# The mixer's input projection: latent blocks and short-convolution blocks in alternation

## What is computed

```python
for i in range(DEPTH):                      # DEPTH = 2
    x = x + 0.5 * swiglu(rmsnorm(x, ffn1_norm[i]), ...)
    h = rmsnorm(x, mix_norm[i]) @ w_in[i]
    y_mla = mla_mixer(h[..., OFF_Q:OFF_KV], h[..., OFF_KV:OFF_KPE], h[..., OFF_KPE:OFF_CONV], ...)
    y_conv = conformer_conv_mixer(h[..., OFF_CONV:OFF_HY], ...)
    y_hy = hyena_mixer(h[..., OFF_HY:], ...)
    y = concatenate([rmsnorm(y_mla, ..), rmsnorm(y_conv, ..), rmsnorm(y_hy, ..)])
    x = x + y @ w_out[i]
    x = x + 0.5 * swiglu(rmsnorm(x, ffn2_norm[i]), ...)
```

## Time and profile before

| what | value |
|---|---|
| median of 3 executions | 3376.35 us (3375.7 to 3377.36) |
| the profiled execution, its own time | 3375.04 us |
| its span, first to last instruction | 3373.2 us |
| mean granted clock of TensorE | 0.972 of full |
| TensorE busy | 3166.9 us, 94% |
| VectorE busy | 1591.3 us, 47% |
| POOL busy | 1881.0 us, 56% |
| ScalarE busy | 697.8 us, 21% |

### The profile page before, as it was taken

One profiled execution on the slowest core, in us unless ns is written; L12 is line 12 of the kernel. 1 busy time (PEld: TensorE's weight loads), 2 busy tenths in 40 slices (PEclk: granted clock), 3 DMA queues, 4 the chain that ended last, 5 costly groups with the idle time before them and its releaser, 6 DMA issues.

```text
span 3373.2 us, 39369 instructions
## 1 busy us (share of the span) xinstructions
PE 3166.9 (94%) x14296; PEld 2413.3 (72%) x14296; DVE 1591.3 (47%) x2395; ACT 697.8 (21%) x1377; POOL 1881.0 (56%) x2079
## 2 busy tenths in 40 slices
PE   6999889989999999998898899997999999999998
PEld 5888665457888788886454688885787666677786
DVE  4312497554312531226857432225665588753424
ACT  2101102251101110011114310013333444420101
POOL 5867670006767777776200377774674423267866
PEclk9999998999999999999899999998999999999999
DMA  3323230002323233233200123232332111123222
GB/s 119 109 84 100 75 123 35 7 1 88 103 91 97 85 99 102 92 100 110 72 7 1 50 88 106 88 100 75 121 92 93 51 45 45 32 76 105 95 87 75
DMA packets 67281, 263.17 MB, mean 78 GB/s; under 512 B 7390, under 2 KB 8606, under 8 KB 65856
## 3 DMA queue, kind: packets, MB, share of 16 engines
q1 hardware_dynamic: 61344, 238.86, 22.0%
q10 hardware_dynamic: 5792, 22.37, 1.8%
HBM read 259.10 MB, written 2.10 MB: 77 GB/s over the span
## 4 chain that ended last, share of the span: by engine, by line
PE 82%; DVE 13%; ACT 2%; issue 2%; POOL 0%; DMA 0%; ACTq 0%; DVEq 0%; SPq 0%; POOLq 0%
PE psum L525 22%; PE psum L527 21%; PE psum L526 21%; DVE y_conv L2046 3%; PE psum L864 2%; PE psum L879 2%; PE psum L822 2%; PE psum L602 1%; PE psum L678 1%; PE psum L628 1%; PE psum L694 1%; PE psum L543 1%; PE psum L756 1%; PE psum L696 1%; PE psum L698 1%
## 5 line engine op out<-in xcount | busy, mean ns | idle before, releaser
L494 POOL TENSOR_TENSOR w_lo<-w_raw,w_hi 128x256 fp32r<-128x256 f32 (+2 forms) x1660 | 1409.8, 880 | 34.6
L489 POOL TENSOR_SCALAR w_hi<-w_raw 128x1024 fp32r<-128x1024 f32 (+2 forms) x415 | 471.3, 1136 | 1435.3 <-PE psum L527 1223.3
L525 PE MATMUL psum<-u_hi,w_hi 128*128 128x512 f32 x2400 | 956.9, 399 | 40.8 <-DVE u_lo L1719 31.1
L526 PE MATMUL psum<-u_lo,w_hi 128*128 128x512 f32 x2400 | 943.8, 393 | 0.0
L527 PE MATMUL psum<-u_hi,w_lo 128*128 128x512 f32 x2400 | 943.4, 393 | 0.0
L525 PEld LDWEIGHTS psum<-u_hi,w_hi 128*128 128x128 f32 x2400 | 456.6, 190 | 169.1 <-issue 52.9
L527 PEld LDWEIGHTS psum<-u_hi,w_lo 128*128 128x128 f32 x2400 | 456.4, 190 | 97.4
L526 PEld LDWEIGHTS psum<-u_lo,w_hi 128*128 128x128 f32 x2400 | 457.5, 191 | 94.7 <-issue 2.9
L525 PE MATMUL psum<-h_hi,w_hi 128*128 128x512 f32 x960 | 374.1, 390 | 4.1 <-issue 4.1
L527 PE MATMUL psum<-h_hi,w_lo 128*128 128x512 f32 x960 | 373.5, 389 | 0.0
L526 PE MATMUL psum<-h_lo,w_hi 128*128 128x512 f32 x960 | 373.5, 389 | 0.0
(11 more groups left out here) (298 smaller groups left out, 3442.3 us busy)
## 6 DMA issues: line engine op xcount, KB each, us to landing
w_raw<-in_w SPq DMA_DIRECT2D x335, 512.0 KB, 3.4
w_raw<-in_w SPq DMA_DIRECT2D x48, 768.0 KB, 4.2
w_raw<-in_w SPq DMA_DIRECT2D x32, 640.0 KB, 3.8
dft<-in_dft ACTq DMA_DIRECT2D x2, 2048.0 KB, 12.6
idft<-in_idft ACTq DMA_DIRECT2D x2, 2048.0 KB, 7.8
w_c<-in_w_c ACTq DMA_DIRECT2D x2, 2048.0 KB
x<-in_xt SPq DMA_DIRECT2D x1, 2048.0 KB, 8.9
decay<-in_decay ACTq DMA_DIRECT2D x2, 1024.0 KB, 7.1
```

Of the source, the lines that this page charges most:

```text
L489: pool.tensor_scalar(hi, raw, 1.0, 1.0, ALU.mult, ALU.mult).then_inc(w_hi_ready, 1)
L494: ins = pool.tensor_tensor(lo[:, part], raw[:, part], hi[:, part].bitcast(F32), ALU.subtract)
L525: pe.matmul(out, hi[:, c, :], rhs_hi(c), start=(s == 0), stop=False)
L526: pe.matmul(out, hi[:, c, :], rhs_lo(c), start=False, stop=False)
```

## The change

A list `W_IN` gives the order of the 14 blocks. The first five stay, then blocks 8, 5, 9, 6, 10, 7 alternate, then 11, 12, 13. The list of loads, TensorE's loop, ScalarE's and VectorE's follow it; what is done with a block goes by its number k as before, what belongs to a place (the wait for the normalized input, the sines) goes by the place `at`. The weights stay where they are in memory.

```diff
+W_IN = (0, 1, 2, 3, 4, 8, 5, 9, 6, 10, 7, 11, 12, 13)
...
     for _ in range(DEPTH):
         ffn(PARTS, 2)
-        add(8, 14)
+        for k in W_IN:
+            out.append((8, first[8] + k, 1))
+        first[8] += len(W_IN)
         add(8, 8)
         ffn(PARTS, 2)
...
-                for k in range(14):
-                    of_u(u_arrives if k == 0 else None)
-                    if k in SINES:
-                        l = SINES.index(k)
+                for at, k in enumerate(W_IN):
+                    of_u(u_arrives if at == 0 else None)
+                    if at in SINES:
+                        l = SINES.index(at)
...
-                for k in range(14):
+                for at, k in enumerate(W_IN):
                     n, m = w.gemm()
                     if 2 <= k < 4:
...
-                    if k in SINES:
-                        l = SINES.index(k)
+                    if at in SINES:
+                        l = SINES.index(at)
...
-                for k in range(14):
+                for at, k in enumerate(W_IN):
                     n, m = w.gemm()
                     if k < 2:
...
-                    if k in SINES:
-                        l = SINES.index(k)
+                    if at in SINES:
+                        l = SINES.index(at)
```

## The result

The changed kernel takes 3382.01 us (median of 20 executions), the kernel before, beside it, 3375.68 (20): ratio 1.0017, with 1.0010 to 1.0024 as its 95% interval. Timed once more later it gave 1.0018 (1.0009 to 1.0027). Two of the 20 executions of the changed kernel were disturbed ones (4075.07 us at a granted clock of 0.742, 12221.04 at 0.423); the median of the other 18 is 3381.7. The change is slower by 0.17%, which lies in the predicted range (3374.0 to 3383.5), under the 0.2% that count here as a change, and on the side that was forecast, but at nearly three times the forecast size: about +6 us against +2.2. The profiled execution took 3380.86 us over a span of 3379.0, where before it took 3375.04 over 3373.2.

A forecast was written before the change was run, and what follows sets the result against it. The prediction took the input projection as a VectorE stage on the chain: +2.75 us of wait less 1.7 saved by overlap with POOL gives +1.1 a layer, +2.2 in all, for 3378.55 us, range 3374.0 to 3383.5.

The forecast's parts named there:

- Step (a): At place 5 VectorE needs a product where it ran six taps without a wait; it idles 2.75 us a layer, unhidden.
- (b): All other new product waits, at places 7, 9 and 11 to 13, are covered because VectorE stays behind TensorE; cost nothing.
- (d): TensorE's own end moves from 498.1 to about 499.5 us, with 12 us of cover before the first filter product; cost nothing.
- Step (c): ScalarE's copies of the latents queue behind the sines, before their banks are wanted by later products; cost nothing.
- Step (e): In the projection, 2.85 us more of POOL's work runs while VectorE can't be slowed by it; saves 1.7 us a layer.
- The first rival: Wait paid in full: taps slow by themselves, or POOL's splits slide; +2.75 us a layer, 3381.85 us, chance 12%.
- The prediction's price: In step (e), each us of POOL's work moved into the shade saves 0.59 us of VectorE's time beside taps.
- The third rival: Faster: the shade is near its upper bound, -1.8 us a layer, 3372.7 us or a little under; chance 4%.
- The second: Slower by TensorE's clock: its rise comes behind the products with ones, 4.0 us more a layer, 3386.5 us; chance 7%.

The follow-up runs named there:

- the change, TensorE's gap filled: Changed kernel with nine unused products in TensorE's gap ahead of its wait for the first sine: 3379.66 us, 1.0013 against the kernel before.
- alternation one block later: Changed kernel with block order 0 to 5, 8, 6, 9, 7, 10 to 13: 3374.94 us, 0.9998 against the kernel before.
- one tap into the wait: Changed kernel with one tap (two VectorE instructions) moved from behind place 5 to place 4, ahead of the wait: 3373.55 us, 0.9996 against the kernel before.
- one tap out of it: Changed kernel with one tap moved from place 4 to behind place 5's short convolution, lengthening the wait: 3381.08 us, 1.0017 against the kernel before.
- in pairs: Changed kernel with block order 0 to 5, 8, 9, 6, 7, 10 to 13: 3373.18 us, 0.9995 against the kernel before.
- the change again: Changed kernel timed once more with no edit: 3380.74 us, 1.0018 against the kernel before.
- before with TensorE's gaps filled: Kernel before with 12 unused products ahead of each of the third and fourth filter products: 3374.45 us, 1.0001 against the kernel before.
- the two doses: Changed kernel with one tap moved into the wait at place 5 (3373.55 us), or one moved out of it (3381.08 us).
- POOL's work cut: Three quarters of the low parts of the input projections' 28 blocks left out: 3358.86 us in the order before, 3365.98 in the changed one.
- pairs and eight: Order 0 to 5, 8, 9, 6, 7, 10 to 13, with one tap instead of two behind each of places 10 to 13: 3361.61 us, 0.9958.

## Why the prediction was right, and where it was off

The frame held: the projection is VectorE's stage, both layers alike, and what happens in it passes on to the end.

Step (a), the wait of 2.75 us at place 5, measured 2.77 and 2.73; the run with one tap in its place shows that it is the cause. Steps (b) and (d): no other product was waited for. TensorE's last block ended near 501.6 instead of 499.5, since place 8 ran at 0.77 of the clock and two later blocks waited for POOL; the cover was over 11 us and still enough. Step (c): each latent was copied 0.5 us behind its sine's start, and no product waited for ScalarE's copy.

Step (e) is where the stretch was mis-sized. It got 1.7 us saved a layer; measured is the wait less the growth, 2.77 - 1.84 = 0.93. The term that failed is its count of the shade, that is of POOL's work done while VectorE idles or reads PSUM. Step (e) had 8.9 us before and 11.75 after. Counted the same way from the two timelines of each run, it was 9.0 and 9.5, so 0.5 us more and not 2.85:

- The wait: 2.0 and not 2.75. Beside an idle VectorE POOL needed 3.59 us for four quarters and not 4.49, was done at 439.6, and stood idle for 0.90 until 440.5.
- The first sine's head (its first instruction, out of PSUM): 0.1 and not 0.5, as POOL waited until 447.2.
- The block near 460: nothing instead of 1.4, as POOL stood still until 463.3.
- The third sine's head: nothing instead of 0.8, as POOL's pause lasted until 483.9.
- Against these, the fifth short block had 2.3 and not 0.9, as POOL's last split came later. Smaller differences make up the rest.

The first rival had named this ("POOL's splits slide so that the shaded time is what it was"), at 12% together with slow taps; for the shade it is nearly what happened. The price of a microsecond in the shade was too low, which made up for part of it. The runs that have POOL's full work and all the taps in the stretch tell both terms apart:

| run | stretch less wait, layer 1 and 2, us | POOL's work in the shade, us |
|---|---|---|
| before | 80.2, 80.1 | 9.0, 9.1 |
| the change | 79.3, 79.1 | 9.5, 9.5 |
| the change, TensorE's gap filled | 78.8, 79.1 | 9.9, 9.7 |
| alternation one block later | 78.7, 78.7 | 10.2, 10.2 |
| one tap into the wait | 78.5, 78.6 | 10.7, 10.7 |
| one tap out of it | 78.1, 77.2 | 10.8, 11.9 |
| in pairs | 78.4, 78.1 | 11.0, 11.1 |

A straight line through these and the two runs left out (the change again, and before with TensorE's gaps filled) falls by 0.9 us for each us of shade and passes within 0.35 us of all of them; it was laid through the results afterwards. The prediction's price was 0.59. By the line the change's 0.5 us of shade give 0.4 of its 0.93; the rest is within the line's spread and stays open. The line also answers the two doses: filling the wait brought 1.2 us of shade besides, as the instructions out of PSUM then had 10.2 us of POOL's work beside them and not 7.5, and lengthening it brought 1.3 and 2.4.

Seen by groups of instructions, the taps gained 2.4 us and the sines lost 1.6. The order moved POOL's splits onto the sines, and step (e) treated everything but their heads as taps. Their one-source instructions in SBUF go from 0.42 us to as much as 1.18 beside POOL, a higher price than a tap's 0.69 to 1.2. How much of the price that was too low is theirs was not tested.

The checkpoints: sines ended at 453.95, 473.33 and 489.50, forecast 453.5, 473.5 and 489.7; the six taps behind the second took 4.52 us (forecast 4.2), those behind the third 6.76 (over 7); the first filter product was taken at 513.05, forecast 512.5. TensorE's waits ahead of the second and third sine's products:

```profile
454.79 1.04 PE L795 MATMUL psum<-f_h,f_w 64*64 64x512 f32 x2 [2.30 <-issue]
...
474.17 1.94 PE L795 MATMUL psum<-f_h,f_w 64*64 64x512 f32 x2 [5.63 <-issue]
```

The first as forecast (2), the second 5.6 and not 7.5, as the block before it came later by the lowered clock.

The rivals. The first (paid in full) did not happen to the stretch, which grew by 1.84 and not by 2.75. Its first mechanism is the rule of the Trainium skill (Vector Engine (DVE) Microarchitecture Reference, section Points that are easy to get wrong) that a scalar-tensor-tensor with two SBUF sources wider than bf16 halves the throughput. This case's traces do not agree: with POOL's work cut ten such taps took 7.99 us instead of 12.14, and alone four took 2.85. That the measured 3382.01 lies beside this rival's 3381.85 is chance, as it is made of other parts. The third rival (faster) had the shade near its upper bound of 16.6; it was 9.5.

The second, the clock in the products with ones, was priced at 4.0 us a layer and given 7%; it came at a tenth and a fifth of that, 0.40 and 0.86, and recurred. With 10.21 and 10.44 us these products lie outside the 9.5 to 10 that the prediction had named as a sign of being wrong. Together with the stretches (3.64 instead of 2.2) and the 0.9 us left over, this makes 5.8 instead of 2.2. The sign came out right by the mechanism that was forecast, the uncovered wait at place 5. The size did not, and that the time still lies in the range is owed to a range wide enough for the full wait and some clock; the term of the clock in the forecast itself was zero, and should not have been.

## What to carry to other kernels

On an engine that holds the chain, moving work that needs a product ahead of work that needs nothing costs about the wait for that product. It can be bought off with work that is already there: one tap moved turned 1.0017 into 0.9996. Where two engines slow each other, look at both timelines and count how much of the other's work falls beside idle time or instructions that it can't slow. In nine runs here that count went with the length of the stretch, and it can't be taken from the old timeline, since each wait moves the other engine's work. An instruction taken off the chain saved about what it takes alone (2.3 to 3.6 us for four, against 2.8), not what it took beside POOL. The larger gain was to do work where another engine holds the chain: 0.9958 for pairs and eight of the stretch's 87 instructions moved behind it, where the pairs alone gave 0.9995.

## What the runs showed of the hardware

Beside POOL's tensor instructions, most of VectorE's instructions with two SBUF sources took 1.1 to 1.2 us instead of 0.7 to 0.75, those with one SBUF source and one SBUF result 0.82 to 1.18 instead of 0.42, and those with a PSUM source did not change (749 to 753 ns). POOL was slowed in turn: four quarters took 4.49 us beside taps and 3.59 where VectorE idled for part of them.

Behind a gap of 2.30 us on TensorE and a small product of 64 rows, the next block ran at a mean clock of 0.77; with the gap filled by products of 128 columns it ran at 1.00, the 2.4 GHz level. In the kernel before, the granted clock was 0.50 from 511.4 to 520.9 us, while TensorE was busy for 7.6 of 9.5 us with filter products of 64 rows, and it rose only within the gapless products with ones, whose mean was 0.76. The same products took 9.8 us at a mean clock of 0.76 and 10.2 at 0.73.
